# Products of the modulation sections cut into four products of 32 weight columns

## The reference, cut to what matters

```
mod = (jax.nn.silu(cond) @ W["mod_w"][l] + W["mod_b"][l])      # (1024) @ (1024, 9 * 1024)
sh1, sc1, g1, sh2, sc2, g2, sh3, sc3, g3 = jnp.split(mod, 9)
x = x + 0.5 * g1 * swiglu_1(rmsnorm(x) * (1 + sc1) + sh1)
x = x + g2 * mixer(rmsnorm(x) * (1 + sc2) + sh2)
x = x + 0.5 * g3 * swiglu_2(rmsnorm(x) * (1 + sc3) + sh3)
```

## Time and profile before

| | |
|---|---|
| median of 3 runs | 3596.19 us (3581.7 to 3600.45) |
| profiled execution, its own time | 3596.85 us |
| span of its records | 3595.1 us |
| mean granted TensorE clock | 0.893 |
| PE busy | 88% of the span |
| DVE busy, ACT busy | 47%, 27% |

### The profile page before, as it was taken

The page is one execution under the profiler, slowest core; times in us unless marked ns, Lnnn a source line. Parts: engine busy times, 40 slices in busy tenths (PEclk is TensorE's granted clock), DMA queues, the critical chain, the costliest instruction groups (busy, mean ns, idle before and its releaser), DMA issues.

```text
span 3595.1 us, 62121 instructions
## 1 busy us (share of the span) xinstructions
PE 3161.0 (88%) x26420; PEld 2965.0 (82%) x26420; DVE 1678.0 (47%) x2611; ACT 982.5 (27%) x1726; POOL 0.2 (0%) x4
## 2 busy tenths in 40 slices
PE   7799999987688877999999999999965555999998
PEld 7799999975566667999999999999942224999998
DVE  2454545553455544554546454544135554432323
ACT  1212123223333322312123212123234343322222
POOL 0000000000000000000000000000000000000000
PEclk6899999986688878999999999999986666999999
DMA  6244433200000002344433444442200001222221
GB/s 216 73 123 112 127 109 98 82 9 0 17 5 4 6 4 77 88 111 123 114 109 93 126 122 120 114 121 73 64 8 5 4 6 50 70 74 78 70 75 60
DMA packets 393659, 264.35 MB, mean 74 GB/s; under 512 B 11627, under 2 KB 375430, under 8 KB 393350
## 3 DMA queue, kind: packets, MB, share of 16 engines
q1 hardware_dynamic: 393478, 261.71, 25.8%
HBM read 257.61 MB, written 4.06 MB: 73 GB/s over the span
## 4 chain that ended last, share of the span: by engine, by line
PE 83%; DVE 10%; ACT 4%; issue 2%; DMA 1%; SPq 0%; DVEq 0%; ACTq 0%
PE pair L2423 61%; PE pair L2446 2%; PE pair L1712 2%; PE pair L2377 1%; PE pair L2432 1%; PE pair L842 1%; PE pair L1707 1%; DVE w_lo_as_f L1821 1%; PE pair L825 1%; PE pair L434 1%; PE pair L409 1%; PE pair L2453 1%; PE pair L897 1%; PE pair L1698 1%; PE pair L836 1%
## 5 line engine op out<-in xcount | busy, mean ns | idle before, releaser
L2423 PE MATMUL pair<-h_hi,w_hi 128*128 128x320 f32 x3600 | 824.2, 310 | 25.0 <-DVE w_lo L2124 25.0
L2423 PE MATMUL pair<-h_lo,w_hi 128*128 128x320 f32 x3600 | 824.1, 310 | 0.0
L2423 PE MATMUL pair<-h_hi,w_lo 128*128 128x320 f32 x3600 | 823.4, 310 | 0.0
L2423 PEld LDWEIGHTS pair<-h_hi,w_hi 128*128 128x128 f32 x3600 | 604.6, 189 | 26.1 <-issue 25.8
L2423 PEld LDWEIGHTS pair<-h_hi,w_lo 128*128 128x128 f32 x3600 | 605.6, 189 | 0.0
L2423 PEld LDWEIGHTS pair<-h_lo,w_hi 128*128 128x128 f32 x3600 | 604.7, 189 | 0.0
L2423 PE MATMUL pair<-big_as_f32r,w_hi 128*128 128x320 f32 x2816 | 538.8, 314 | 5.3 <-DVE w_lo L2124 4.1
L2124 DVE TENSOR_TENSOR w_lo<-raw,w_hi 128x1024 fp32r<-128x1024 f32 x333 | 398.8, 1219 | 215.7 <-ACT w_hi L2008 214.8
L2008 ACT ACTIVATE w_hi<-raw 128x1024 fp32r<-128x1024 f32 x333 | 342.0, 1051 | 470.0 <-DMA raw<-ffn_w 256.6
L2423 PEld LDWEIGHTS pair<-big_as_f32r,w_hi 128*128 128x128 f32 x2816 | 451.3, 192 | 6.7 <-DVE w_lo L2124 4.9
L2269 DVE TENSOR_TENSOR work<-work,pair 128x640 f32<-128x640 f32 x88 | 72.2, 821 | 620.6 <-PE pair L2423 606.5
(11 more groups left out here) (359 smaller groups left out, 3077.7 us busy)
## 6 DMA issues: line engine op xcount, KB each, us to landing
raw<-ffn_w SPq DMA_DIRECT2D x272, 512.0 KB, 5.2
work<-mod_w SPq DMA_DIRECT2D x136, 512.0 KB, 3.8
raw<-w_in_c SPq DMA_DIRECT2D x24, 512.0 KB, 3.8
raw<-w_in_ab SPq DMA_DIRECT2D x21, 512.0 KB, 3.9
w_hi_as_f<-mod_w SPq DMA_DIRECT2D x8, 512.0 KB, 4.6
raw<-w_out_ab SPq DMA_DIRECT2D x8, 512.0 KB, 5.1
raw<-w_out_c SPq DMA_DIRECT2D x8, 512.0 KB, 5.6
h_hi_as_f<-x_sample SPq DMA_DIRECT2D x1, 2048.0 KB
```

The source lines that it names most:

```text
L2423: ins = nc.tensor.matmul(ps[:, c, 0:HALF], w, v[:, k, c * HALF:(c + 1) * HALF], start=(k == 0 and w is hi and v is xh), stop=(k == kts - 1 ...
```

## The change

Each of the 16 products of a section becomes four, for weight columns 0 to 31, 32 to 63, 64 to 95 and 96 to 127 of its tile, with the outputs in the same 32 partitions of the same PSUM column. All 128 rows, the column of ones and every number computed stay the same. A section has 64 products in place of 16, 960 in all in place of 240. The order of the stages, the loads, the semaphores and the other engines' code are untouched.

```
                     for t in range(DT):
                         for g in range(2):
                             c = HALF + 2 * t + g
-                            ins = nc.tensor.matmul(ps[:, 1, c:c + 1], sec_sum[:, q % 2, g, t * P:(t + 1) * P], ones,
-                                                   start=True, stop=True)
+                            for r in range(0, P, 32):
+                                ins = nc.tensor.matmul(ps[r:r + 32, 1, c:c + 1], sec_sum[:, q % 2, g, t * P + r:t * P + r + 32],
+                                                       ones, start=True, stop=True)
                 ins.then_inc(slab_used, 1)
```

## The result

The changed kernel takes 3541.7 us (median of 4 runs, 3539.58 to 3543.7) against 3591.85 us before (4 runs, 3581.7 to 3600.45): ratio 0.9853, 95% interval 0.9832 to 0.9875.

A forecast was written before the change was run, and what follows sets the result against it. PE was taken to bound the kernel. From the profiled 3596.85 us, −21.0 for shorter sections and −8.2 for fewer clock falls gave 3567.7, or 3567.0 us on the median's scale; range 3554 to 3609 us.

The forecast's parts named there:

- PE sets the pace at the sections, and what they give goes to the end one for one: At the sections PE is busy throughout, so any time saved there shortens the whole span equally.
- Places work side by side, and a place's pass costs by its columns: Section products: output quarters load weights in parallel; a 32-column pass costs its place about 0.03 us.
- Opening and closing the places: 0.24 and 0.14 us: Section edges: 0.24 us from last slab matmul to first product, 0.14 from last product to next slab.
- I take 0.0146, the fastest sustained, as the cost of getting them issued: Spacing of 32-column passes in a section: 0.0146 us, giving 2.23 us a section in place of 3.63.
- The term of 21.0 us: Saving in the sections' own time: 1.40 us less in each of 15 sections, −21.0 us.
- Row (c): Profile row of products 64 by 64 in four places by turns, 0.0146 us a pass; source of the assumed spacing.
- The rule of about 25 ns from start to start: Rival for the section products: matmuls never start closer than about 25 ns; 3.56 us a section, 3595 us, chance 0.17.
- The falls, scaled by length: 7 left of 11, −8.2 us: Clock halvings after sections, assumed proportional to section length: 6.8 remain of 11, saving 8.2 us.
- no falls left: Best case for the clock after sections: it never drops to half, saving 21 us.
- the rate of 0.008: Lower bound for a section's passes: 0.008 us each if only parallel loading binds, −33 us in all.
- Instructions: Fetching the 2880 added PE records: costed at nothing; +18 us if every section had to wait for a packet.
- the price kept beside it: Fallback cost of an instruction wait at a section: 1.2 us each, from the instruction queue's packets.

## Why the prediction missed the range

*PE sets the pace at the sections, and what they give goes to the end one for one.* Right: 53 us counted in the sections and behind them, and the three stretches that hold the sections are 52 us shorter.

*Places work side by side, and a place's pass costs by its columns.* Right, with its number: 0.0294 us measured in one place, "about 0.03" expected, and the gain is gone when neighbours share a place.

*Opening and closing the places: 0.24 and 0.14 us.* Right: 0.24 ahead, and behind, from the last pass (238.14 + 1.24 − 0.17 = 239.21) to 239.31, 0.10. In six sections 0.13 to 0.30 us come on top, for which the sum had no term.

*"I take 0.0146, the fastest sustained, as the cost of getting them issued."* This is the step that put the time outside the range, whose lower end of 3554 had the falls gone already and passes at 0.0146. The term of 21.0 us was mis-sized; it measured 32. A pass measured 0.0084 us, so 0.0146 is no floor of issuing. Row (c) is explained by loading, 0.058 us for a place over four places: the same argument by which 0.008 came out as the lower bound. The 0.0146 should have been an upper bound alone. The measured 0.0084 is just above 0.0074, a quarter of a place's pass.

*The rule of about 25 ns from start to start* (the Trainium skill, "TensorE: Matmul & The Clock Gate", section "Wait — 56ns, not 53.3ns?"). The trace of the changed kernel agrees with neither count of it: passes start 8.4 ns apart, and products of two passes 17.

*The falls, scaled by length: 7 left of 11, −8.2 us.* The second term that was mis-sized, and by as much: none left, so 21 us by the same estimate, where 8.2 were put. The scaling had no row behind it; by the table above the falls do go with length, but not in proportion. It was made for a run of 1.85 us of passes; the run was 1.07. At 1.84 us, with 64 columns, 4 were left, at 1.59 none. The bound "no falls left" was on record.

With both terms at their bounds, −33 and −21, the sum would have been 3596.85 − 54 = 3543, against 3542.14 measured. The range left out the rate of 0.008 "for which no row stands", and the two ends together were never put in it. That this sum comes within 1 us is in part luck, as the mixer of layer 0 happened to take the same time in both executions.

*Instructions.* Costed at nothing, and right: in the changed kernel's trace no two passes of a section start more than 0.033 us apart. But the price kept beside it, 1.2 us for each wait, was only the time that one packet moves. A wait, where the run was three times as long, measured 1.0 to 6.0 us, 88 us in 29 stops.

## What to carry to other kernels

A sum over the partitions with one moving column is paid by its weight columns. Cut into products for different quarters of the output partitions, and ordered so that neighbours use different quarters, it ran 3.2 times faster here (1.07 against 3.38 us from first to last start), and in the wrong order slower than whole. Count the passes of a straight stretch before doing so: 128 went through in all 15 sections, and beyond 142 to 258, by section, PE waited 1.0 to 6.0 us for its next packet of instructions. Where one stage of the same code varies from execution to execution, as the mixer did here, compare the stages that hold the change. And where the trace shows a floor, ask whether another limit in the same row explains it whole; then it is no floor.

## What the runs showed of the hardware

- Passes of 128 rows by 32 columns with one moving column: 0.0084 us apart in four places by turns, 0.0294 in one place; 64 columns in two places 0.029; all at a granted clock of 1.00.
- Straight code of such passes stopped after 142 to 258 passes and then after 128 more (256 records, one packet of 16.4 KB); PE went on 1.2 to 1.6 us after the packet had landed.
- The step from matmuls of 128 columns to passes of 32 columns took 0.24 us from start to start (0.15 to products of 128 columns), the step back 0.10 us (0.11).
- After runs of one-column matmuls of 1.07 us the clock fell in none of 75 cases, after 1.59 us in none of 15, after 3.38 us in 11 of 15, and a matmul of 192 moving columns ahead of each product did not prevent it.
